# Moving the second norm's token factor behind the second in-projection

## The reference

```python
# end of the first block
x = x + einsum(gelu(gate) * up, w_down)          # the down stage
x = rms_norm(x, final_g)                         # the norm at the seam: x * rstd(token) * final_g(channel)
# second block
h = x @ w_in                                     # the second in-projection
x_q, x_kv, k_rope_raw, gate_a, u_pool, gate_b = split(h)
y_a = mla(rms_norm(x_q) @ w_uq, rms_norm(x_kv) @ w_ukv, rope(k_rope_raw)) * silu(gate_a)
y_b = pool_branch(u_pool) * silu(gate_b)         # windows of 2, 4, 8, 16 tokens
x = layer_norm(alpha * x + concat(y_a, y_b) @ w_out, ln_g, ln_b)
```

## Time and profile before

| what | value |
|---|---|
| median of 3 runs | 1730.13 us (1728.16 to 1732.98) |
| profiled execution, first to last instruction | 1726.5 us |
| its own time, not listed apart from its span | not known; the median of the runs lies 3.6 us above the span |
| PE busy | 1681.0 us, 97% |
| DVE, ACT, POOL busy | 71%, 46%, 30% |
| mean granted PE clock | 0.992 |

### The profile page before, as it was taken

How to read it: one execution, slowest core, us unless ns; L and a number is a source line. 1 busy time by engine, 2 the same in 40 slices (tenths; PEclk the granted TensorE clock), 3 DMA queues, 4 the chain that set the end, 5 groups by cost and what they waited for, 6 DMA issues and landing times.

```text
span 1726.5 us, 20915 instructions
## 1 busy us (share of the span) xinstructions
PE 1681.0 (97%) x7556; PEld 1383.3 (80%) x7556; DVE 1225.3 (71%) x1442; ACT 792.4 (46%) x1038; POOL 516.6 (30%) x284
## 2 busy tenths in 40 slices
PE   7999999999999999999999999998999999999998
PEld 6888878888877888888888888886878877777776
DVE  6577772259999888888888789885636365666554
ACT  5466541235764434343434455553322146676531
POOL 4221222200015555554552000003432242345320
PEclk8999999999999999999999999999999999999999
DMA  8111112152422232222223876651321320110251
GB/s 259 49 36 49 40 45 74 37 201 80 152 81 76 83 97 73 84 84 87 73 86 125 317 237 199 219 159 43 122 74 61 85 86 25 37 49 25 102 215 73
DMA packets 161095, 176.96 MB, mean 102 GB/s; under 512 B 13566, under 2 KB 114692, under 8 KB 161028
## 3 DMA queue, kind: packets, MB, share of 16 engines
q1 hardware_dynamic: 158724, 167.67, 30.3%
q10 hardware_dynamic: 2304, 8.39, 1.3%
HBM read 140.38 MB, written 35.65 MB: 102 GB/s over the span
## 4 chain that ended last, share of the span: by engine, by line
PE 82%; DVE 10%; ACT 4%; issue 1%; POOL 1%; DMA 1%; POOLq 0%; DVEq 0%; ACTq 0%; SPq 0%
PE ps L921 28%; PE ps L2398 24%; PE ps L2352 18%; PE ps L2618 4%; PE ps L2603 3%; PE ps L2648 2%; PE ps L2588 1%; DVE lat L2109 1%; PE ps L2576 1%; DVE pt_lo L2203 1%; DVE prob L2185 1%; POOL z_lo L1015 1%; PE ps L2279 1%; DVE square_dve L1636 0%; ACT pt_hi L1548 0%
## 5 line engine op out<-in xcount | busy, mean ns | idle before, releaser
L945 POOL TENSOR_TENSOR w_lo<-w_raw,w_hi 128x1024 fp32r<-128x1024 f32 x52 | 135.8, 2614 | 623.0 <-ACT w_hi L1044 623.0
L2398 PE MATMUL ps<-hop_hi_P,wop_hi_P 128*128 128x512 f32 x672 | 262.5, 391 | 4.7 <-DVE u L1853 3.3
L2398 PE MATMUL ps<-hop_hi_P,wop_lo_P 128*128 128x512 f32 x672 | 261.5, 389 | 0.0
L2398 PE MATMUL ps<-hop_lo_P,wop_hi_P 128*128 128x512 f32 x672 | 261.5, 389 | 0.0
L921 PE MATMUL ps<-h_hi,w_hi 128*128 128x512 f32 x752 | 235.1, 394 | 11.3 <-DVE h_lo L1621 7.8
L951 POOL TENSOR_TENSOR wop_lo_P<-pair_sum,wop_hi_P 128x512 fp32r<-128x512 f32 x90 | 135.9, 1510 | 354.5 <-ACT wop_hi_P L1055 354.5
L921 PE MATMUL ps<-h_lo,w_hi 128*128 128x512 f32 x752 | 232.9, 391 | 0.0
L921 PE MATMUL ps<-h_hi,w_lo 128*128 128x512 f32 x752 | 232.7, 391 | 0.0
L921 PEld LDWEIGHTS ps<-h_hi,w_hi 128*128 128x128 f32 x752 | 141.4, 189 | 43.3 <-issue 14.0
L921 PEld LDWEIGHTS ps<-h_lo,w_hi 128*128 128x128 f32 x752 | 142.1, 189 | 29.8
L921 PEld LDWEIGHTS ps<-h_hi,w_lo 128*128 128x128 f32 x752 | 142.0, 189 | 29.7
(11 more groups left out here) (350 smaller groups left out, 3337.9 us busy)
## 6 DMA issues: line engine op xcount, KB each, us to landing
pair_raw<-in_w_up SPq DMA_DIRECT2D x48, 512.0 KB, 4.6
w_raw<-in_w_in SPq DMA_DIRECT2D x46, 512.0 KB, 3.9
dn_raw<-gu_park SPq DMA_DIRECT2D x84, 256.0 KB, 3.9
dn_raw<-in_w_down SPq DMA_DIRECT2D x60, 256.0 KB, 3.1
gu_park<-up_cv SPq DMA_DIRECT2D x24, 512.0 KB, 2.6
out_raw<-in_w_out SPq DMA_DIRECT2D x30, 256.0 KB, 3.0
x_tok<-in_x SPq DMA_DIRECT2D x4, 1024.0 KB, 8.2
x_park<-xs SPq DMA_DIRECT2D x1, 4096.0 KB, 14.3
```

The lines of the kernel that those rows point to most:

```text
L945: nc.gpsimd.tensor_tensor(lo[:, :], raw[:, :], hi[:, :].bitcast(f32), ALU.subtract).then_inc(w_lo_done, 1)
L2398: mm = nc.tensor.matmul(dst, w[q][:, k, :], x[q][:, k, :], start=a, stop=b, skip_group_check=True)
```

## The change

The token factor no longer goes into the inputs of the second in-projection. The inputs become `final_g * xs`, made by DVE in place, half tile by half tile (`final_gains`), and split by ACT (`final_high`) and by DVE and POOL (`final_low`) in the order `FINAL_TURNS`: the eight T1 halves, then T2 of tiles 4 to 7 and 0 to 3. PE runs the T1 halves of blocks N_IN2 and N_IN2+1 right after the down stage, then `mean_squares`, then the T2 halves, with `spread` within those of the first block. The spread factor is copied to a tile, `rstd3`, by ACT, and multiplies the sums of each block afterwards: in place of the copies of `lat` and `u`, and as new instructions of DVE for the four `gate_b`, the four `gate_a` and the rope keys, ahead of ACT's tanh or swaps. The parked residual takes ALPHA*rstd as the scale. `by_token` now stands behind each block N_IN2 + 2..5 and not ahead of it, and `park_residual` one turn later.

```diff
+            def final_low(c, t):
+                pool.wait_ge(hi_done, 8 + final_turn(c, t))
+                nc.gpsimd.tensor_tensor(h_lo[:, c, t], xs[:, c, t], h_hi[:, c, t].bitcast(f32),
+                                        ALU.subtract).then_inc(lo_pool, 1)
...
-            odd_lows(1, lambda c: xs[:, c, :])
+            for c, t in FINAL_TURNS:
+                if c % 2 == 1:
+                    final_low(c, t)
...
             high(N_IN2)
+            for c in range(4):
+                final_high(c, T1)
             high(N_IN2 + 1)
             for j in range(12, 16):
                 square(DOWN, j)
+                final_high(j - 8, T1)
+            for c in range(4, KT):
+                final_high(c, T2)
             norm_root(3)
-            highs(lambda c: xs[:, c, :], lambda c: (v_done, 24 + c + 1))
+            for c in range(4):
+                final_high(c, T2)
+            act.wait_ge(rb_done, 3)
+            nc.scalar.copy(rstd3[:, :], ps[1][:, :]).then_inc(rstd3_spread, 1)
+            act.wait_ge(rstd3_scaled, 1)
...
-                if 1 <= i <= NT // 2:
-                    park_residual(2 * i - 2)
-                    park_residual(2 * i - 1)
+                if i >= 2:
+                    park_residual(2 * i - 4)
+                    park_residual(2 * i - 3)
...
-                act.wait_ge(block_done, read(N_POOL + 2 * g + 1))
+                act.wait_ge(gb_scaled, g + 1)
                 nc.scalar.activation(y_pool[:, g, :], ps[1][:, :], ACT.Tanh, scale=0.5).then_inc(th_done, 1)
                 high(N_POOL + 2 * g + 3)
...
             def gate(h):
-                act.wait_ge(block_done, read(N_GATE + h))
+                act.wait_ge(ga_scaled, h + 1)
...
             high(N_KR + 2)
+            act.wait_ge(kr_scaled, 1)
             swap_halves(0, ps[0])
...
-            for p in range(4):
-                last_block(DOWN, p)
-                add_square(DOWN, 12 + p)
+            dve.wait_ge(x1_square, DOWN.square(12))
+            final_gains(FINAL_TURNS[0:8])
+            last_block(DOWN, 0)
+            final_low(0, T1)
+            final_low(2, T1)
+            last_block(DOWN, 1)
+            add_square(DOWN, 12)
+            final_low(4, T1)
+            final_gains(FINAL_TURNS[8:12])
+            last_block(DOWN, 2)
+            add_square(DOWN, 13)
+            final_low(6, T1)
+            last_block(DOWN, 3)
+            add_square(DOWN, 14)
+            final_low(4, T2)
+            final_low(6, T2)
+            add_square(DOWN, 15)
+            final_gains(FINAL_TURNS[12:16])
             dve.wait_ge(root_done, 3)
             V.reciprocal(rstd[:, :], small[:, 8:16]).then_inc(rstd_done, 1)
-            dve.wait_ge(rb_done, 3)
-            norm(1, V_FINAL, lambda c: xs[:, c, :], ps[3][:, :], False)
+            final_low(0, T2)
+            final_low(2, T2)
...
-                V.tensor_copy(lat[:, i, :], ps[i % 2][:, :]).then_inc(lat_done, 1)
+                V.tensor_tensor(lat[:, i, :], ps[(2 + i if i < 2 else i % 2)][:, :], rstd3[:, :], ALU.mult).then_inc(lat_done, 1)
...
-                V.tensor_copy(scr[0][:, :], ps[0][:, :]).then_inc(u_done, 1)
+                V.tensor_tensor(scr[0][:, :], ps[0][:, :], rstd3[:, :], ALU.mult).then_inc(u_done, 1)
...
                     V.reciprocal(scale[:, :], scale[:, :]).then_inc(rstd2_done, 1)
+                dve.wait_ge(block_done, read(N_POOL + 2 * g + 1))
+                V.tensor_tensor(ps[1][:, :], ps[1][:, :], rstd3[:, :], ALU.mult).then_inc(gb_scaled, 1)
...
             def gate(h):
+                dve.wait_ge(block_done, read(N_GATE + h))
+                V.tensor_tensor(ps[h % 2][:, :], ps[h % 2][:, :], rstd3[:, :], ALU.mult).then_inc(ga_scaled, 1)
...
             dve.wait_ge(block_done, read(N_KR))
+            V.tensor_tensor(ps[0][:, :], ps[0][:, :], rstd3[:, :], ALU.mult).then_inc(kr_scaled, 1)
...
+            for k in range(8 + 3):
+                for b, j in ((0, k), (1, k - 3)):
+                    if 0 <= j < 8:
+                        final_step(b, j, T1, j == 0, j == 7)
             pe.wait_ge(x1_squares, squared(DOWN, 16))
-            mean_squares(scr[4], ps[2]).then_inc(ms_done, 1)
-            pe.wait_ge(rstd_done, 3)
-            spread(ps[3]).then_inc(rb_done, 1)
+            mean_squares(scr[4], ps[0]).then_inc(ms_done, 1)
+            for b in range(2):
+                for k in (4, 5, 6, 7, 0, 1, 2, 3):
+                    if b == 0 and k == 2:
+                        pe.wait_ge(rstd_done, 3)
+                        spread(ps[1]).then_inc(rb_done, 1)
+                    final_step(b, k, T2, k == 4, k == 3)
...
-            first_two(N_IN2, (ps[0], ps[1]), 1)
-            pe.wait_ge(v_done, 32)
+            pe.wait_ge(rstd3_spread, 1)
             for i in range(2, Q_TILES + KV_TILES):
+                if i >= 4:
+                    pe.wait_ge(lat_done, i - 1)
+                project(N_IN2 + i, 0, ps[i % 2], h_hi, h_lo)
+                if i == 2:
+                    pe.wait_ge(final_gain, 16)
+                    pe.wait_ge(lat_done, 2)
                 by_token(2 * i - 4)
                 by_token(2 * i - 3)
-                pe.wait_ge(lat_done, i - 1)
-                project(N_IN2 + i, 0, ps[i % 2], h_hi, h_lo)
```

More of the change, by code:

```diff
@@ L260, in program @@
         pooled_lo = tile("pooled_lo", G0, 12, f32r)
-        square2 = tile("square2", G0, 13)
+        square2 = tile("square2", G0, 7)
+        rstd3 = tile("rstd3", G0, 13)
         y_pool = tile("y_pool", X0, 0, f32, 4)
@@ L394, in program @@
         rstd_spread = sem("rstd_spread")
+        final_gain, rstd3_spread, rstd3_scaled = sem("final_gain"), sem("rstd3_spread"), sem("rstd3_scaled")
+        gb_scaled, ga_scaled, kr_scaled = sem("gb_scaled"), sem("ga_scaled"), sem("kr_scaled")
         tok_t, tok_copied = sem("tok_t"), sem("tok_copied")
@@ L568, in program, with final_turn, final_low_turn @@
         rstd_row = xs[:, 4:6, T2]
+        FINAL_TURNS = tuple((c, T1) for c in range(KT)) + tuple((c, T2) for c in (4, 5, 6, 7, 0, 1, 2, 3))
+        def final_turn(c, t):
+            return FINAL_TURNS.index((c, t)) + 1
+        def final_low_turn(c, t):
+            return sum(x % 2 == c % 2 for x, _ in FINAL_TURNS[:final_turn(c, t)])
         def stream_bank(q, p):
@@ L985, in _ @@
             low(N_IN2 + 1)
-            odd_lows(1, lambda c: xs[:, c, :])
+            pool.wait_ge(slice_lo, DOWN.split(DOWN.steps - 1))
+            pool.wait_ge(product_added, DOWN.added(10))
+            for c, t in FINAL_TURNS:
+                if c % 2 == 1:
+                    final_low(c, t)
             nc.gpsimd.memset(acc_q[:, :], 0.0).then_inc(acc_q_done, 1)
@@ L1298, in norm_root @@
                 act.wait_ge(ms_done, n)
-                src = ps[2][:, HALF:HALF + NT] if n == 2 else ps[2][:, 0:NT]
+                src = ps[2][:, HALF:HALF + NT] if n == 2 else ps[0][:, 0:NT]
                 nc.scalar.activation(small[:, 8:16], src, ACT.Sqrt, bias=eps[:, 0:1]).then_inc(root_done, 1)
@@ L1406, in _, with final_high @@
                     square(DOWN, 8 + n - 80)
+            def final_high(c, t):
+                act.wait_ge(final_gain, final_turn(c, t))
+                nc.scalar.copy(h_hi[:, c, t], xs[:, c, t]).then_inc(hi_done, 1)
             high(N_IN2)
+            for c in range(4):
+                final_high(c, T1)
             high(N_IN2 + 1)
@@ L1418, in park_residual @@
                     act.wait_ge(res_parked[t % 2], 16 * (t // 2))
-                nc.scalar.mul(scr[t % 2][:, :], ps[2 + t % 2][:, :], ALPHA).then_inc(tok_copied, 1)
+                nc.scalar.activation(scr[t % 2][:, :], ps[2 + t % 2][:, :], ACT.Identity, scale=small[:, t:t + 1]
+                                     ).then_inc(tok_copied, 1)
                 act.wait_ge(tok_copied, t + 1)
@@ L2023, in _, with final_gains, final_low @@
                     add_square(DOWN, 8 + n - 80)
-            for p in range(4):
-                last_block(DOWN, p)
-                add_square(DOWN, 12 + p)
+            def final_gains(turns):
+                for c, t in turns:
+                    V.tensor_scalar(xs[:, c, t], xs[:, c, t], col(V_FINAL + c), None, ALU.mult).then_inc(final_gain, 1)
+            def final_low(c, t):
+                dve.wait_ge(hi_done, 8 + final_turn(c, t))
+                V.tensor_tensor(h_lo[:, c, t], xs[:, c, t], h_hi[:, c, t].bitcast(f32), ALU.subtract).then_inc(lo_dve, 1)
+            dve.wait_ge(x1_square, DOWN.square(12))
[16 more added lines that the diff above has]
+            final_gains(FINAL_TURNS[12:16])
             dve.wait_ge(root_done, 3)
             V.reciprocal(rstd[:, :], small[:, 8:16]).then_inc(rstd_done, 1)
-            dve.wait_ge(rb_done, 3)
-            norm(1, V_FINAL, lambda c: xs[:, c, :], ps[3][:, :], False)
+            final_low(0, T2)
+            final_low(2, T2)
+            dve.wait_ge(rstd_done, 3)
+            V.tensor_scalar(small[:, 0:8], rstd[:, :], ALPHA, None, ALU.mult).then_inc(rstd3_scaled, 1)
```

(22 more changed lines are left out.)

## The result

The changed kernel takes 1742.89 us (median of 4 runs, 1741.16 to 1743.95) against 1730.56 for the kernel before (1728.16 to 1732.98): slower by a ratio of 1.0066, with a 95% interval of 1.0049 to 1.0084. The forecast was 1740.5 us in a range of 1732 to 1746. The profiled execution took 1743.95 us with a span of 1742.2; the kernel before had 1728.16 and 1726.5. The profiled run of before is the shortest of its four and that of after the longest, so the two profiled executions lie 15.7 us apart (by their spans) and the medians 12.3.

A forecast was written before the change was run, and what follows sets the result against it. PE, busy 97% of the 1726.5 us span, was taken as the bound. Terms -3.1 (seam and latents), +5.6, +4.6, +0.1 and +3.2 (clock) sum to +10.4 on 1730.1, giving 1740.5 us, range 1732 to 1746.

The forecast's parts named there:

- rival 3: At the seam DVE's list is later and the clock falls again, nothing of the 3.1 left; +15, 1745 us; chance 0.13.
- seam, to the end of the first two blocks: From the down stage to the end of N_IN2+1: block ends at 1201.8, 7.8 us ahead of before.
- latents, to the start of N_POOL: Second in-projection: waits for latent 1, residual copies and 3.0 us ahead of N_POOL leave 3.1 of the 7.8 us gained.
- wait for `pooled_lo`, g = 1: Pool part: multiplication stands behind DVE's reciprocal, tanh and its queue follow, PE waits; +5.6 us (4.5 to 5.7).
- wait at N_KR: Gate 2's multiplication follows the latents' low parts, so tanh, cast and `w_lo` end later; +4.6 us (4.3 to 4.8).
- half clock behind these waits: After the pool-part and N_KR stalls PE runs at half clock; 1.6 us each, +3.2 us (0 to 4.8).
- behind N_KR: Gates 0, 3 and N_KR: multiplication hidden under ACT's weight cast or PE's next block; +0.1 us in all.
- The hand-made passage through three queues: Seam lists of DVE, ACT and POOL, engines hindering each other: last low halves and sum of squares late, 2.6 us lost.
- The two queues behind the tanh: Pool part g = 1 and gate 2: casts and splits queued behind a delayed tanh make PE wait; +5.6 and +4.6 us.
- That the clock holds (1): Same stalls in the pool part and at N_KR, but full clock stays: +7.2, 1737 us; chance 0.22.
- That the engines hardly hinder each other (2): POOL and DVE hinder each other little at the seam, stalls take lower bounds: +3.3, 1733.5 us; chance 0.15.
- The faster kernel (4): Queues behind tanh do not hold PE up, `pooled_lo` of g = 1 under 2.0 us later: 1725 to 1727; chance 0.05.

The follow-up runs named there:

- experiment 8: Changed kernel plus 24 matmuls of 512 columns, their result unread, in PE's wait for N_KR's low weights; 1739.87 us, ratio 1.0041 to the kernel before.
- Experiment 4: Changed kernel with the eight T1 gain multiplications spread over the last eight steps of the down stage; 1740.64 us, ratio 1.0053 to the kernel before.
- Experiment 3: Changed kernel with PE waiting for the eighth residual copy behind block N_POOL, not ahead of it; 1736.13 us, ratio 1.0035 to the kernel before.
- experiment 5: Changed kernel with VectorE's sine and cosine arguments one turn later, after latents 1 and 2; 1738.43 us, ratio 1.0038 to the kernel before.
- Experiments 1: Changed kernel with ACT's weight cast in the pool part ahead of its wait for gb_scaled and the tanh; 1735.64 us, ratio 1.0025 to the kernel before.
- experiment 2: Changed kernel with ACT's weight cast in the gate part ahead of its wait for ga_scaled and the tanh; 1737.41 us, ratio 1.0038 to the kernel before.
- experiment 6: Changed kernel with the five edits of experiments 1 to 5 together; 1718.51 us, ratio 0.9912 to the kernel before.
- experiment 7: Kernel of experiment 6 with gate 2's product ahead of the latents' low parts and N_KR's cast and split earlier; 1714.08 us, ratio 0.9894 to the kernel before.

## Why the prediction was right

**The sign and the size.** Forecast +10.4, measured +12.3 by the medians. The mechanism was the one forecast: a gain at the seam, eaten up by three queues behind it. Term by term, by the two profiles, the sum is +15.6, and 5.2 more than forecast. The profiles lie 3.4 us further apart than the medians, of which the seam's clock can explain 1.6; the rest is open. So that the time came out within 2.4 us of 1740.5 is in part luck: the forecast was short in the clock and in the seam, and the medians show less of it than the profiles. The time lies between the forecast and rival 3 (1745), as near to one as to the other.

| term | forecast | measured |
|---|---|---|
| seam, to the end of the first two blocks | -7.8 | -5.6 (-7.2 where the clock held) |
| latents, to the start of N_POOL | +4.7 | +4.9 |
| wait for `pooled_lo`, g = 1 | +5.6 | +5.3 |
| wait at N_KR | +4.6 | +4.6 (6.6 less 2.0) |
| half clock behind these waits | +3.2 | +6.4 |
| behind N_KR | +0.1 | none to be seen |

**The seam.** The hand-made passage through three queues put the low halves of tiles 6 and 7 last, PE's waits at 0.2 and 1.8 us, and the sum of squares 0.5 after PE wanted it. The profile has 0.7, 1.5 and 0.2, which is 2.4 us in all where the forecast lost 2.6. From the end of the down stage's splits to the end of the two blocks the forecast was 40.5 us (1201.8 less 1161.34); 41.0 to 41.1 were measured in four profiles, 42.7 in the changed kernel's own and in that of experiment 8. In the changed kernel's own the clock stood at 0.59 and 0.80 in the 5.7 us behind the token sums. That DVE and GpSimd keep each other waiting shows in these lines of the changed kernel's timeline. Unhindered, the eight gains would follow each other every 0.40 us, as four of them do at 1189.21 (1.66 us), and be done in 3.3 us:

```profile
1164.38 5.40 DVE L2066 TENSOR_SCALAR xs<-xs,vec 128x512 f32<-128x512 f32 x8
...
1170.32 4.47 DVE L2071 TENSOR_TENSOR h_lo<-xs,h_hi 128x512 fp32r<-128x512 f32 x2
...
1164.61 2.52 POOL L958 TENSOR_TENSOR w_lo<-w_raw,w_hi 128x1024 fp32r<-128x1024 f32 x1 [233.75 <-ACT w_hi L1067]
1170.14 2.40 POOL L958 TENSOR_TENSOR w_lo<-w_raw,w_hi 128x1024 fp32r<-128x1024 f32 x1 [3.01 <-ACT w_hi L1067]
1172.50 3.44 POOL L977 TENSOR_TENSOR h_lo<-xs,h_hi 128x512 fp32r<-128x512 f32 x2
```

The gains take 2.1 us too long beside GpSimd's first split. Two low halves in 4.47 us, beside its second, are the same again; a low half alone takes 0.69. Experiment 4, which moves the eight to where GpSimd is idle, removes PE's waits for `h_lo`, so their lateness was the cause. How much of it was the meeting with GpSimd and how much the 3.3 us of passes themselves was not taken apart: experiment 4 moves both at once, and its two low halves still take 4.33 us.

**Latents.** The new wait of 3.2 ahead of N_POOL (forecast 3.0), of 1.4 for latent 1 (1.1) and of 2.2 for the copies (2.9) came much as read from the order of the lists. Experiment 3 shows that the first was no need of N_POOL at all; experiment 5 that the others came from sine and cosine.

**The two queues behind the tanh.** They were right to 0.3 us, because each could be added up from rows: the wait of the moved pass for DVE, and everything that ACT and GpSimd have listed behind it. Experiments 1 and 2 leave every pass in and remove the waits by changing only who stands behind the tanh. One point of the reading was too simple: at N_KR the product of gate 2 was late too (PE free at 1412.9, the product done at 1417.3, `w_lo` at 1419.4), hidden behind `w_lo`, and became the wait once `w_lo` came earlier.

**The clock was the mis-sized term.** The forecast priced two stalls at 1.6 us each, 3.2 with bounds of 0 to 4.8, and gave the wait of 3.0 us no price and no reason for it. All three waits paid, and the 6.4 lie above its bounds: the stretch from N_POOL to the end of N_POOL+2 grew by 1.7, the one from there to the end of gate 1 by 7.9, of which 5.3 is the wait and 2.6 the clock, and the rest of the path by 2.1 more than the waits. That is 6.4. Experiment 8 confirms the last of them as clock: 2.1 us. The Trainium skill ("TensorE: Matmul & The Clock Gate", "HAM oscillation") has a loop fall to the lower clock at each of its DMA waits; here the waits are for other engines, and the trace agrees for those of 3.2, 5.3 and 6.6 us, all followed by 0.50.

**The rivals.** That the clock holds (1) is refuted by the rows at 0.50. That the engines hardly hinder each other (2) does not fit 5.40 us for eight passes, and the seam gave 5.6 to 7.2 us, not 10.3. The worse seam (3) came half true, through the clock. The faster kernel (4) failed at the point named: `pooled_lo` ended 15.4 us after the reciprocal's start in place of 8.0, so 7.4 later and not under 2.0. A kernel faster than before by this change is what experiments 6 and 7 then built.

## What to carry to other kernels

In this kernel, a multiplication moved behind a product cost little where nothing that PE needed soon stood behind its consumer in that engine's list, and far more than its own length where something did: before such a move, write down for each new wait what is queued behind it on the same engine, and add up its slack. Here 1.2 us passes turned into 5.3 and 4.6 us of added wait; exchanging two lines, once in the pool part and once in the gate part, took back all of the first and 4.2 of the second. And a change that looks like a loss can be a gain with unfinished orders: the same factor, with the six edits of experiment 7, ends 18 us below the kernel before, of which roughly two thirds are its own.

## What the runs showed of the hardware that was not expected

The clock's fall is not tied to one length of wait. Waits of 3.2, 5.3 and 6.6 us were followed by half speed in the changed kernel, and by a block of 12.5 us or more in place of 10.9 wherever the 3.2 or the 6.6 stood in another profile. Waits of 1.8 to 2.4 us were followed by it in some and not in others: N_KR's wait of 2.4 us left the clock at 1.00 in experiment 2 and let it fall in experiment 6 (0.57 over the 4 us behind it), and the wait of 1.8 us for `qh_lo`, which all eleven profiles have, let it fall in experiment 4 alone (a block of 12.8 us, and of 11.1 to 11.2 in the ten others). In that case the drop came 1.6 us after PE had started again:

```profile
1464.53 0.70 PE L934 MATMUL ps<-kvn_hi,w_hi 128*128 128x512 f32 x2 [1.79 <-DVE qh_lo L2213]
1465.07 0.63 PE L934 MATMUL ps<-kvn_lo,w_hi 128*128 128x512 f32 x2
1465.54 0.84 PE L934 MATMUL ps<-kvn_hi,w_lo 128*128 128x512 f32 x2
1466.17 1.05 PE L934 MATMUL ps<-kvn_hi,w_hi 128*128 128x512 f32 x2
```

So a single profile can show 1.6 us more or less at a place that no edit touches. The seam is such a place too: with the same code there, the changed kernel and experiment 8 read -5.6 us, and experiments 1, 2, 3 and 5 read -7.2.
